# A three-layer fp32 network on one core: who makes the low parts of the third layer's weights, and where they stand among its rotations, softmaxes and norms

## The reference

```python
h = rmsnorm_2(x, norm_mix_g[l])
proj = h @ w_in[l]
q, k, v, gu, gv, gate_a, gate_b = jnp.split(proj, splits, axis=-1)
q = rope(q.reshape(B, S, MOBA_HEADS, MOBA_HD))
k = rope(k.reshape(B, S, MOBA_HEADS, MOBA_HD))
...
y_a = moba_attention(q, k, v) @ moba_w_proj[l]
y_b = gmlp_spatial_gating(gu, gv, gmlp_norm_g[l], gmlp_w_s[l], gmlp_b_s[l]) @ gmlp_w_proj[l]
merged = jax.nn.sigmoid(gate_a) * y_a + jax.nn.sigmoid(gate_b) * y_b
x = x + merged @ w_out[l]
h = rmsnorm_2(x, norm_xa_g[l])
m = rmsnorm_2(mem, norm_mem_g[l])
x = x + memory_cross_attention(h, m, xa_w_q[l], xa_w_kv[l], xa_w_o[l])
h = rmsnorm_2(x, norm_ffn_g[l])
x = x + peer_ffn(h, peer_w_q[l], peer_subkeys[l], peer_w_down[l], peer_w_up[l])
```

## Time and profile before

| | |
|---|---|
| median of 3 runs | 2101.07 us (2098.35 to 2104.29) |
| the profiled execution | 2107.43 us, of which the span of instructions is 2105.6 us |
| PE busy | 1950.6 us (93%) |
| PEld busy | 1796.8 us (85%) |
| DVE busy | 1354.4 us (64%) |
| ACT busy | 986.3 us (47%) |
| POOL busy | 333.6 us (16%) |
| mean granted TensorE clock | 0.965 |
| chain that ended last, by engine | PE 72%, DVE 15%, ACT 3%, issue 2%, POOL 1%, DMA 1% |

### The profile page before, as it was taken

The page is one execution under the profiler, slowest core; times in us unless marked ns, Lnnn a source line. Parts: engine busy times, 40 slices in busy tenths (PEclk is TensorE's granted clock), DMA queues, the critical chain, the costliest instruction groups (busy, mean ns, idle before and its releaser), DMA issues.

```text
span 2105.6 us, 33493 instructions
## 1 busy us (share of the span) xinstructions
PE 1950.6 (93%) x13340; PEld 1796.8 (85%) x13340; DVE 1354.4 (64%) x2482; ACT 986.3 (47%) x1431; POOL 333.6 (16%) x151
## 2 busy tenths in 40 slices
PE   5889799988998789998898889899999999999998
PEld 5877699987977589997897879899998888999997
DVE  4897665556955764335643146988878887666665
ACT  5444454453434354445444445566663333444444
POOL 1001044430001024440006537200000000000000
PEclk9999999998999899999999999999999999999999
DMA  7653366654644245554344334467776776554553
GB/s 292 238 180 126 130 220 243 238 189 172 214 172 174 82 162 199 180 184 165 137 140 141 116 105 161 155 192 225 213 218 234 268 267 231 200 221 180 200 185 116
DMA packets 94234, 392.82 MB, mean 187 GB/s; under 512 B 7648, under 2 KB 41584, under 8 KB 55552
## 3 DMA queue, kind: packets, MB, share of 16 engines
q1 hardware_dynamic: 94080, 390.69, 53.2%
HBM read 372.83 MB, written 15.73 MB: 185 GB/s over the span
## 4 chain that ended last, share of the span: by engine, by line
PE 72%; DVE 15%; ACT 3%; issue 2%; POOL 1%; DMA 1%; DVEq 0%; SPq 0%; ACTq 0%
PE ps L565 9%; PE ps L567 9%; PE ps L566 9%; PE acc L561 8%; PE acc L562 8%; PE acc L563 8%; DVE wlo L1270 3%; PE acc L565 2%; PE acc L566 2%; PE acc L567 2%; DVE arena L1299 2%; PE ps L628 1%; PE acc L1225 1%; PE ps L1225 1%; DVE arena L1466 1%
## 5 line engine op out<-in xcount | busy, mean ns | idle before, releaser
L2261 ACT ACTIVATE whi<-raw 128x1024 fp32r<-128x1024 f32 x559 | 588.9, 1059 | 530.7 <-PE acc L563 282.5
L1270 DVE TENSOR_TENSOR wlo<-raw,whi 128x1024 fp32r<-128x1024 f32 x430 | 530.2, 1241 | 304.0 <-ACT whi L2261 303.5
L565 PE MATMUL ps<-hhi,whi 128*128 128x256 f32 x1880 | 541.1, 288 | 21.2 <-DVE wlo L1270 10.0
L566 PE MATMUL ps<-hlo,whi 128*128 128x256 f32 x1880 | 536.0, 285 | 0.0
L567 PE MATMUL ps<-hhi,wlo 128*128 128x256 f32 x1880 | 535.7, 285 | 0.0
L1270 POOL TENSOR_TENSOR wlo<-raw,whi 128x1024 fp32r<-128x1024 f32 x129 | 316.6, 2459 | 650.8 <-ACT whi L2261 650.5
L565 PEld LDWEIGHTS ps<-hhi,whi 128*128 128x128 f32 x1880 | 364.6, 194 | 28.2 <-issue 7.3
L566 PEld LDWEIGHTS ps<-hlo,whi 128*128 128x128 f32 x1880 | 364.8, 194 | 2.9
L567 PEld LDWEIGHTS ps<-hhi,wlo 128*128 128x128 f32 x1880 | 364.5, 194 | 0.0
L561 PE MATMUL acc<-whi,chi 128*128 128x512 f32 x752 | 298.6, 397 | 9.9 <-DVE wlo L1270 8.4
L562 PE MATMUL acc<-whi,clo 128*128 128x512 f32 x752 | 296.5, 394 | 0.0
(11 more groups left out here) (449 smaller groups left out, 2449.5 us busy)
## 6 DMA issues: line engine op xcount, KB each, us to landing
raw<-in_peer_down SPq DMA_DIRECT2D x64, 1024.0 KB, 4.9
raw<-in_peer_up SPq DMA_DIRECT2D x64, 1024.0 KB, 5.0
arena<-in_ada SPq DMA_DIRECT2D x80, 512.0 KB, 4.9
raw<-in_w_gate SPq DMA_DIRECT2D x22, 1024.0 KB, 4.8
raw<-in_w_up SPq DMA_DIRECT2D x22, 1024.0 KB, 5.0
raw<-in_w_down SPq DMA_DIRECT2D x22, 1024.0 KB, 4.8
arena<-spill SPq DMA_DIRECT2D x14, 1024.0 KB, 6.9
spill<-hT_t SPq DMA_DIRECT2D x22, 448.0 KB, 5.8
```

Source lines behind the costliest of these rows:

```text
L565: e.matmul(out, hi, xh, start=start, stop=False, skip_group_check=True)
L566: e.matmul(out, hi, xl, start=False, stop=False, skip_group_check=True)
L1270: e.tensor_tensor(out=lo, in0=w, in1=hi.bitcast(F32), op=ALU.subtract).then_inc(*X(("lo", j)))
L2261: e.activation(hi, w, ACT.Copy, scale=1.0).then_inc(*self.A(("hi", j)))
```

## The change

1. **Low parts.** `lo_engine` no longer gives the seven weights named above to GpSimd; all 32 blocks go to VectorE, where they stand wherever `ve_cuts` or `cut_lo` comes to them.
2. **Rotations.** Each rotation is cut in two: three of the four 32-row products, then (one product of TensorE later) the fourth with the cosine and the sum. The first starts one product later than it did, and the four pieces lie behind the cuts of `w_mqk` 2, `w_mqk` 3, `w_gu` 0 and `w_gu` 1.
3. **Softmaxes.** One block's cut stands between the maxima and the scaling of the probabilities on VectorE (ahead of the exponentials on ScalarE), and for the moba attention the next block's cut right behind the softmax, ahead of the gating. For the second softmax the first of these is made already between the transposes and the heads of the first.
4. **The memory's norm.** Its squares and roots on ScalarE go into the loop of `gmlp_proj` (with the table load ahead of it); VectorE's part goes there and into the loop of `moba_proj`. TensorE's part stays where it was.
5. **Sums into x.** `ve_sum` starts the first half's norm before the last sum, and one block's cut may lie in it; `ve_out` and `se_out` of `w_out2` go one block less far.

```diff
@@ lo_engine
-        if name in ("gmlp_proj", "moba_proj", "w_out2", "xa_k", "xa_v", "xa_q", "xa_o"):
-            return "G"
         return "G" if (name, i, half) in FIRST else "V"
@@
+    def moba_at(self, qt):
+
+        return self.W.last("w_gab", 63) if qt else self.W.last("w_mv", 15, 256)
@@ ve_sum
-        for tt in range(2):
-            for half in range(2):
-                self.ve_add_x(e, post, tt, half)
-        for tt in range(2):
-            self.ve_eps(e, norm, tt, 48)
-            self.ve_diag(e, norm, tt)
...
+        self.ve_add_x(e, post, 0, 0)
+        self.ve_add_x(e, post, 0, 1)
+        self.ve_add_x(e, post, 1, 0)
+        self.ve_eps(e, norm, 0, 48)
+        self.ve_diag(e, norm, 0)
+        self.ve_add_x(e, post, 1, 1)
+        if ahead is not None:
+            self.cut_lo(e, self.V, ahead)
+        self.ve_eps(e, norm, 1, 48)
+        self.ve_diag(e, norm, 1)
@@ ve_scores, between the loop of the maxima and that of the scaling
+        if ahead is not None:
+            self.cut_lo(e, V, ahead)
@@ ve_mix2 (the rotation's body goes into ve_rope)
         for i in range(4):
             self.ve_linear(e, "w_mqk", i, 8, 2)
-            if i % 2:
...
+            if i > 1:
+                self.ve_rope(e, 0, i - 2)
         for i in range(2):
             self.ve_linear(e, "w_gu", i, 8, 2)
+            self.ve_rope(e, 1, i)
@@
+    def ve_rope(self, e, which, part):
...
+        for r in ((0, 32, 64), (96,))[part]:
...
+        if part:
+            for r in (0, 32, 64, 96):
+                e.wait_ge(*self.at("turned_by", which, r))
+            e.tensor_tensor(out=x, in0=x, in1=bc(m.cos2.unsqueeze(1), [128, 4, T]), op=ALU.mult).then_inc(*V())
+            e.wait_ge(*V.last)
+            e.tensor_tensor(out=x, in0=x, in1=m.rot2, op=ALU.add).then_inc(*V(("moba_rope", which)))
@@ ve_moba
+            at = self.moba_at(qt)
             self.ve_scores(e, f"moba{qt}", 8, nk, 0.125, lambda hs, n: bc(m.cb2[:, 256 - nk:256].unsqueeze(1), [128, n, nk]),
-                           m.St2)
+                           m.St2, ahead=at + 3)
+            self.cut_lo(e, V, at + 4)
             if qt == 0:
                 self.ve_gmlp(e)
...
             self.ve_turn(e, f"moba{qt}", 8, nk, m.PT2)
+            if qt == 0:
+                self.cut_lo(e, V, self.moba_at(1) + 3)
             self.ve_bank_split(e, f"moba{qt}", m.cH, m.cL, qt)
@@ in the loop of gmlp_proj, then of moba_proj
+            if i % 2:
+                self.ve_eps(e, "mem", i // 2, 48)
...
+            if i < 2:
+                self.ve_diag(e, "mem", i)
@@ behind w_out2 0 to 3
-        for tt in range(2):
-            self.ve_eps(e, "mem", tt, 48)
-            self.ve_diag(e, "mem", tt)
...
-        self.ve_out(e, "w_out2", range(4, 8))
+        self.ve_out(e, "w_out2", range(4, 8), 1)
@@ ve_xa
-        self.ve_sum(e, "w_out2", "xa")
+        self.ve_sum(e, "w_out2", "xa", self.W.last("w_out2", 63) + 2)
...
-        self.ve_scores(e, "xa", 8, 256, 128.0 ** -0.5, None, m.St2)
+        self.ve_scores(e, "xa", 8, 256, 128.0 ** -0.5, None, m.St2, ahead=self.W.last("xa_q", 31) + 3)
@@ se_norm
             self.se_root(e, nm, tt, at)
+            if tt == 0 and ahead is not None:
+                self.cut_hi(e, ahead)
@@ se_moba
+            at = self.moba_at(qt)
+            self.cut_hi(e, at + 3)
             self.se_scores(e, f"moba{qt}", 8, nk, m.St2)
+            self.cut_hi(e, at + 4)
...
+            if qt == 0:
+                self.cut_hi(e, self.moba_at(1) + 3)
             self.se_bank_split(e, f"moba{qt}", m.cH, qt)
+        e.preload_act_table_set(LOG_SET)
+        e.wait_ge(self.landed["mem"], 16)
         for i in range(4):
             self.se_linear(e, "gmlp_proj", i, 4, 2)
+            self.se_square(e, "mem", m.mem[:, i // 2, 512 * (i % 2):512 * (i % 2) + 512], i // 2, i % 2, 48)
+            if i % 2:
+                self.se_root(e, "mem", i // 2, 48)
...
-        e.preload_act_table_set(LOG_SET)
-        e.wait_ge(self.landed["mem"], 16)
-        self.se_norm_of(e, "mem", m.mem)
```

More of the change, by code:

```diff
@@ L1428, in ve_add_x, with ve_sum, ve_scores @@
             *V(("x", nm, tt, half), ("out", nm, "acc", 2 * tt + half)))
-    def ve_sum(self, e, post, norm):
-        for tt in range(2):
-            for half in range(2):
-                self.ve_add_x(e, post, tt, half)
-        for tt in range(2):
-            self.ve_eps(e, norm, tt, 48)
-            self.ve_diag(e, norm, tt)
-    def ve_scores(self, e, nm, nh, nk, scale, bias, St, gate=None):
+    def ve_sum(self, e, post, norm, ahead=None):
+        self.ve_add_x(e, post, 0, 0)
[8 more added lines that the diff above has]
+        self.ve_diag(e, norm, 1)
+    def ve_scores(self, e, nm, nh, nk, scale, bias, St, gate=None, ahead=None):
         m, V = self.m, self.V
@@ L1921, in ve_mix2 @@
             self.ve_linear(e, "w_mqk", i, 8, 2)
-            if i % 2:
-                x = (m.mq, m.mk)[i // 2]
-                e.wait_ge(*self.at("out", "w_mqk", i))
-                if i == 3:
-                    e.wait_ge(*self.at("moba_rope", 0))
-                for r in (0, 32, 64, 96):
-                    r2 = r ^ 32
-                    e.tensor_tensor(out=m.rot2[r2:r2 + 32, :, :], in0=x[r:r + 32, :, :],
-                                    in1=bc(m.sin2[r:r + 32, :].unsqueeze(1), [32, 4, T]), op=ALU.mult).then_inc(*V())
-                e.wait_ge(*V.last)
-                e.tensor_tensor(out=x, in0=x, in1=bc(m.cos2.unsqueeze(1), [128, 4, T]), op=ALU.mult).then_inc(*V())
-                e.wait_ge(*V.last)
-                e.tensor_tensor(out=x, in0=x, in1=m.rot2, op=ALU.add).then_inc(*V(("moba_rope", i // 2)))
+            if i > 1:
+                self.ve_rope(e, 0, i - 2)
         for i in range(2):
             self.ve_linear(e, "w_gu", i, 8, 2)
+            self.ve_rope(e, 1, i)
         for i in range(2):
@@ L1947, in ve_mix2 @@
                                    op0=ALU.mult, op1=ALU.mult).then_inc(*V(*([("gmlp_v",)] if tt else [])))
+    def ve_rope(self, e, which, part):
+        m, V = self.m, self.V
+        x = (m.mq, m.mk)[which]
+        if part == 0:
+            e.wait_ge(*self.at("out", "w_mqk", 2 * which + 1))
+            if which:
+                e.wait_ge(*self.at("moba_rope", 0))
+        for r in ((0, 32, 64), (96,))[part]:
+            r2 = r ^ 32
+            e.tensor_tensor(out=m.rot2[r2:r2 + 32, :, :], in0=x[r:r + 32, :, :],
+                            in1=bc(m.sin2[r:r + 32, :].unsqueeze(1), [32, 4, T]), op=ALU.mult).then_inc(
+                                *V(("turned_by", which, r)))
+        if part:
[4 more added lines that the diff above has]
+            e.tensor_tensor(out=x, in0=x, in1=m.rot2, op=ALU.add).then_inc(*V(("moba_rope", which)))
     def ve_gmlp(self, e):
@@ L2339, in se_junction, with se_norm @@
         self.se_root(e, norm, 1, 48)
-    def se_norm(self, e, nm, src, at=48):
+    def se_norm(self, e, nm, src, at=48, ahead=None):
         for tt in range(2):
@@ L2705, in se_moba @@
         self.se_out(e, "w_out2", range(4))
-        e.preload_act_table_set(LOG_SET)
-        e.wait_ge(self.landed["mem"], 16)
-        self.se_norm_of(e, "mem", m.mem)
         self.cut_hi(e, self.W.last("w_out2", 31) + 3)
         self.se_normed(e, "mem", m.pv("g_mem2"), None, None, m.cH)
-        self.se_out(e, "w_out2", range(4, 8))
+        self.se_out(e, "w_out2", range(4, 8), 1)
     def se_xa(self, e):
         m, A = self.m, self.A
-        self.se_norm(e, "xa", "w_out2")
+        self.se_norm(e, "xa", "w_out2", ahead=self.W.last("w_out2", 63) + 2)
         for i in range(2):
@@ L2722, in se_xa @@
             self.se_linear(e, "xa_q", i, 8, 2, m.mk[:, 2 * i:2 * i + 2, :])
+        self.cut_hi(e, self.W.last("xa_q", 31) + 3)
         self.se_scores(e, "xa", 8, 256, m.St2)
```

## The result

The changed kernel takes 2065.76 us (median of 4 runs, 2064.47 to 2067.08) against 2101.55 us before (4 runs, 2098.35 to 2104.29): a ratio of 0.9837, 95% interval 0.9817 to 0.9858, so 35.8 us less. The forecast was 2067.0, from a sum of 34.2 us.

The account below looks back on a forecast made before the run. TensorE, busy 93%, was taken as the bound: time is won only where it waits or runs at half clock. Eight terms sum to 34.2 us, 2101.07 - 34.2 = 2067 us; range 2062 to 2077 (65%), 8 in 10: 2057 to 2081.

Parts of the forecast that it names:

- the walk: Step-by-step reckoning of when VectorE has each low part ready against when TensorE needs it, in the new order.
- Rotations: At `w_mqk` and `w_gu`: two waits of 3.67 us and a half-clock stretch of 1.3 behind each go; 10.0 us.
- First softmax: 3.65 us wait at `w_gab1` goes, 1.7 comes back at `w_gab2`, plus 1.3 for the clock; 3.2 us.
- Second softmax: 2.96 us wait and 2.8 of double half clock go, 0.3 comes back at the following block; 5.5 us.
- Merging: At `w_out2`: three turns win 0.3 us each as low parts move to VectorE, start slightly better; 1.1 us.
- Memory's norm: TensorE's 2.12 us wait for the diagonal matrix goes, and 1.3 for the clock; 3.5 us.
- term 4: The merging at `w_out2`, 1.1 us; its start was to hold the memory norm's 2.7 us of ScalarE work.
- Waits for GpSimd: Five small waits vanish (1.9 us), the long one at `xa_k` shrinks 0.5, half its clock returns 0.6; 3.0 us.
- Cross attention's softmax: Heads start 3.4 us sooner, as the last scalings shorten, and run at full clock, 1.9; 5.3 us.
- Norm behind: Norm behind the cross attention: 1.4 of the 1.88 us wait for its diagonal goes, 1.2 for the clock; 2.6 us.
- the first of them: Rival, 20%: half is given back, VectorE's in-order waits hold up work behind them; 21 us saved, 2081 us.
- More than I count: Rival, 8%: waits at `w_out2`, `xa_k` and the new 1.7 us one vanish too; 42 us saved, 2059 us.

Follow-up runs that it names:

- e2: Kernel before with only the two rotations split in two and standing one product later; 2092.07 us, ratio 0.9962.
- e4: Changed kernel with the rotations whole and back where they were; 2077.64 us, ratio 0.9879.
- e7: Changed kernel with the gating's high and low part moved behind the work for `w_gab1`; 2064.22 us, ratio 0.9826.
- e3: Changed kernel with the low parts of the seven weights back on GpSimd; 2074.02 us, ratio 0.9880.
- e5: Changed kernel without the high and low parts made in and right behind the three softmaxes; 2074.15 us, ratio 0.9885.
- e1: Kernel before with only the low parts of the seven weights given to VectorE; 2088.42 us, ratio 0.9939.
- e8: Changed kernel with the next high and low parts made inside the merging's cycle, on ScalarE and VectorE; 2061.82 us, ratio 0.9817.
- e6: Changed kernel with the memory's norm back behind the first half of `w_out2`; 2069.83 us, ratio 0.9844.
- e9: Changed kernel with two of `peer_q`'s low parts on VectorE and one high part fewer ahead of the norm's; 2066.41 us, ratio 0.9821.
- e12: Changed kernel with later gating parts, weight parts inside the merging's cycle, and `peer_q`'s two low parts on VectorE; 2057.90 us, ratio 0.9795.

## Why the prediction was right, term by term

The mechanism held: the waits went where the walk said, what was left stood where it said, but for 0.3 us at `w_gab5` that did not come and 0.97 at `peer_q` that did, and the clock stayed up. That the time came within 1.3 us of the forecast is in part luck. The ledger has 3.2 us more than the sum of 34.2, over half of it in one term, and two terms are right because errors in them cancel.

- *Rotations, 10.0: 10.45 us.* The walk held to the end. There is no wait; at `w_gmv`, where the lead was forecast to shrink to 0.3, two matmuls start 0.33 us apart in place of 0.12. The sum took 1.3 us for each half-clock stretch; it costs 1.5 (last section). The 1.3 came of dividing a stretch of 3.4 us by the 31 matmuls that the view counts in it, the overlapping ones at its ends included; the twelve lost ones at the prediction's own pace of 0.12 are 1.4. e2 and e4 show that this part stands by itself.
- *First softmax, 3.2: 3.41.* The old wait of 3.65 went and the new one came, at `w_gab2`, 1.72 us against 1.7 said, for the reason given: e7 takes ScalarE's table load off that way, and it goes. The row's way was right: the load begins 0.02 us behind the gating's high part and the next ACTIVATE 0.01 behind the load. The Trainium skill, "ScalarE: Activation LUTs", What ACT_TABLE_LOAD costs, books a drain of about 1.38 us beside the load, which by the prediction's estimate would have made the wait 3.1; these rows have no room for one. ScalarE's rows in the changed kernel:

```profile
1035.37 1.06 ACT L2719 ACTIVATE chi<-arena 128x1024 fp32r<-128x1024 f32 x1 [3.88 <-DVE arena L1982]
1036.45 1.28 ACT L2297 ACT_TABLE_LOAD   x1
1037.74 0.60 ACT L2297 ACTIVATE arena<-acc 128x512 f32<-128x512 f32 x1
```

- *Second softmax, 5.5: 5.51.* e3 and e5 show the mechanism: the early place of the parts carries it. The exact number is luck. The half clock of double length was booked at 2.8 and is worth 2.55 (e1 has the wait without it), and the 0.3 that should have come back at `w_gab5` did not: 2.96 + 2.55 = 5.51.
- *Merging, 1.1: 1.4.* The waits are 1.10, 1.21 and 1.20 against 1.4 said, VectorE's cycle 4.2 against 4.3. The row on VectorE and GpSimd (2.52 us for a sum that takes 0.69 alone) held in e3 too: 2.51. The Trainium skill, "SBUF — State Buffer", SBUF: two separate sides, says that GpSimd and an instruction of VectorE with two inputs in SBUF lock the port pair that they share, each for its whole instruction, while the other is blocked; e3's rows agree (2.51 beside 0.69). But the lock was not the price of the stage: without it the cycle went from 4.6 to 4.2 us only, and e8 takes another 4.25 us from the stage by the order of the work.
- *Memory's norm, 3.5: 4.0,* most of it as said (its two parts, 2.1 and 1.3, make 3.4, not 3.5); e6 splits it. The norm's place gives 1.4 net of the 1.0 that it costs the merging, so "its cost is in the start of term 4" named the right place, and the size is 1.0.
- *Waits for GpSimd, 3.0: 4.80.* The one term that is off by more than 0.5. `xa_k`'s wait fell to 1.96 (0.65 less; 0.5 said). The clock there, booked at half of 1.3, did not fall, which is 1.5. The rest is small stops: 4.80 - 0.65 - 1.5 = 2.65 us. Only four of the five lie in this stage (0.28, 0.43, 0.43 and 0.43, together 1.57 us); the fifth, of 0.28, stands behind it, in `xa_o`.
- *Cross attention's softmax, 5.3: 5.29.* Heads at 1189.03 with a wait of 1.42, in 3.81 us at full clock. e1, e5 and e3 show what the forecast did not: the low parts on VectorE alone give the 3.4 and the early place alone 2.7, so these two gains don't add.
- *Norm behind, 2.6: 2.52.* The first wait fell to 0.52, as said. The rest is right by cancelling: the clock was worth 1.5 and not 1.2 and the fifth small stop went here, but the wait at `peer_q` grew from 0.31 to 0.97. That tail, not in the forecast, is GpSimd's and goes in e9.

None of the rivals came (the first of them, 2101.07 less 21 us, is 2080 and not the 2081 written). "More than I count" was nearest in kind: its waits are real, and e12 took two of the three, but VectorE had to be given the work in another order first.

## What to carry to other kernels

Where the busiest engine waits in several stages for an in-order engine, write the due time of each piece beside its ready time for the whole stage: terms worked out that way fell within 0.5 us here, seven of eight, two of them with luck. Two edits that take the same wait away must not be booked twice: undo each in the finished kernel as well as doing each alone (low parts: 14.6 us alone, 2.55 of them clock, and 7.6 undone). And look for an idle gap of the waited-for engine inside its own cycle (here VectorE waiting for ScalarE's high part): filling it, in two lines, won 4.25 us at the merging, where the whole change had won 1.4.
